# Index scores from the longest row of keys to the shortest, with each mask added at its tile

## The reference, cut to what matters

```python
logits = jnp.einsum('bqhd,bkd->bqhk', qi, k_idx_f)
score = jnp.einsum('bqh,bqhk->bqk', wi, jax.nn.relu(logits))
score = jnp.where(s_pos[None, None, :] <= t_pos[None, :, None], score, -jnp.inf)
_, idx = lax.top_k(score, topk)
```

## Time and profile before

| | us |
|---|---|
| median of 3 runs | 3659.33 (3657.73 to 3661.23) |
| the profiled execution, its own time | 3661.77 |
| the profiled execution, span of the trace | 3660.0 |
| TensorE busy in the span | 3364.4 |
| VectorE busy in the span | 1764.8 |

### The profile page before, as it was taken

How to read it: one execution, slowest core, us unless ns; L and a number is a source line. 1 busy time by engine, 2 the same in 40 slices (tenths; PEclk the granted TensorE clock), 3 DMA queues, 4 the chain that set the end, 5 groups by cost and what they waited for, 6 DMA issues and landing times. The chain is left out here.

```text
span 3660.0 us, 39794 instructions
## 1 busy us (share of the span) xinstructions
PE 3364.4 (92%) x15224; PEld 2696.9 (74%) x15224; DVE 1764.8 (48%) x2726; ACT 1115.5 (30%) x1955; POOL 579.7 (16%) x401
## 2 busy tenths in 40 slices
PE   7999888876989899999999998988899899999998
PEld 5776666665777587888888776776666688888886
DVE  4425544457341435555554539789543423242334
ACT  4323333325232322122111424136675321111212
POOL 0002365642100001010000200000164201000010
PEclk8999999988999999999999999999999999999999
DMA  4232323230321004332221301123233111111111
GB/s 122 75 101 84 118 78 115 87 134 15 117 68 65 37 20 133 98 97 97 97 80 48 133 18 41 46 56 84 67 67 114 39 58 47 46 52 50 47 46 58
DMA packets 223493, 270.27 MB, mean 74 GB/s; under 512 B 17259, under 2 KB 150276, under 8 KB 221298
## 3 DMA queue, kind: packets, MB, share of 16 engines
q1 hardware_dynamic: 223348, 268.30, 23.6%
HBM read 219.68 MB, written 29.18 MB: 68 GB/s over the span
## 5 line engine op out<-in xcount | busy, mean ns | idle before, releaser
L193 PE MATMUL psum<-rounded,rounded 128*128 128x512 f32 (+2 forms) x3936 | 1540.7, 391 | 115.6 <-DVE rounded L222 51.3
L194 PE MATMUL psum<-rounded,rounded 128*128 128x512 f32 (+2 forms) x3936 | 1530.5, 389 | 0.0
L195 PE MATMUL psum<-rounded,rounded 128*128 128x512 f32 (+2 forms) x3936 | 1529.1, 388 | 0.0
L193 PEld LDWEIGHTS psum<-rounded,rounded 128*128 128x128 f32 x3936 | 748.1, 190 | 293.1 <-DVE rounded L222 56.5
L195 PEld LDWEIGHTS psum<-rounded,rounded 128*128 128x128 f32 x3936 | 747.7, 190 | 152.4
L194 PEld LDWEIGHTS psum<-rounded,rounded 128*128 128x128 f32 x3936 | 749.0, 190 | 148.8 <-issue 0.2
L2966 DVE TENSOR_TENSOR plain<-psum,plain 128x512 f32<-128x512 f32 x432 | 288.2, 686 | 110.7 <-PE psum L195 109.1
L2977 DVE TENSOR_TENSOR plain<-psum,plain 128x512 f32<-128x512 f32 x44 | 30.4, 691 | 424.1 <-ACT plain L2881 424.1
L3538 POOL TENSOR_TENSOR plain<-plain,plain 128x128 f32<-128x128 f32 (+3 forms) x64 | 96.9, 1523 | 591.4 <-ACT plain L3636 516.0
L3343 DVE TENSOR_SCALAR_CACHE_REDUCE plain<-plain,plain 128x384 bf16<-128x384 f32 (+2 forms) x204 | 181.8, 942 | 1.3
L2958 DVE TENSOR_TENSOR rounded<-plain,rounded 128x512 fp32r<-128x512 f32 x108 | 97.2, 900 | 164.8 <-ACT rounded L2870 164.6
(11 more groups left out here) (327 smaller groups left out, 3467.1 us busy)
## 6 DMA issues: line engine op xcount, KB each, us to landing
plain<-in_ff_w_dram SPq DMA_DIRECT2D x64, 512.0 KB, 5.4
plain<-in_w_ada_dram SPq DMA_DIRECT2D x96, 256.0 KB, 3.3
plain<-in_w_gu_dram SPq DMA_DIRECT2D x44, 512.0 KB, 4.9
plain<-in_w_in_dram SPq DMA_DIRECT2D x36, 512.0 KB, 4.0
rounded<-rounded SPq DMA_DIRECT2D x72, 256.0 KB, 3.4
plain<-in_c_fwd_dram SPq DMA_DIRECT2D x64, 256.0 KB, 2.6
plain<-in_w_down_dram SPq DMA_DIRECT2D x22, 512.0 KB, 3.7
fold<-plain SPq DMA_DIRECT2D x8, 1024.0 KB, 5.0
```

Source lines behind the costliest of these rows:

```text
L193: nc.tensor.matmul(out, wh, xh, start=first, stop=False)
L194: nc.tensor.matmul(out, wh, xl, start=False, stop=False)
L195: return nc.tensor.matmul(out, wl, xh, start=False, stop=last)
```

## The change

The list of steps runs over the tiles from 7 down to 2. The zeros and the mask of tiles 0 and 1 are written by VectorE at the block's start, before it waits for the heads' weights. The mask of each other tile is added right behind its eighth head, after a wait for that head's addition.

```diff
-    steps = [(i, h) for i in range(FIRST_SEL, TT) for h in range(8)]
+    steps = [(i, h) for i in reversed(range(FIRST_SEL, TT)) for h in range(8)]
...
         @block.vector
         def _(dve):
+            for i in range(FIRST_SEL):
+                sc = sel_tile(core, i)
+                if i:
+                    nc.vector.memset(sc[:, 0:i * P], 0.0)
+                nc.vector.tensor_copy(sc[:, i * P:], core.small[:, 4, :])
             dve.wait_ge(S["tr_done"].sem, S["tr_done"].at(1))
...
                 ins.then_inc(S["dve_done"].sem, 1)
-            dve.wait_ge(S["dve_done"].sem, S["dve_done"].at(len(steps)))
-            for i in range(TT):
-                sc = sel_tile(core, i)
-                if i < FIRST_SEL:
-                    if i:
-                        nc.vector.memset(sc[:, 0:i * P], 0.0)
-                    nc.vector.tensor_copy(sc[:, i * P:], core.small[:, 4, :])
-                else:
+                if h == 7:
+                    dve.wait_ge(S["dve_done"].sem, S["dve_done"].at(n + 1))
                     nc.vector.tensor_tensor(sc[:, i * P:], sc[:, i * P:], core.small[:, 4, :], ALU.add)
```

## The result

| | before | changed |
|---|---|---|
| median of 18 runs, us | 3662.44 (3657.15 to 3667.61) | 3667.79 (3665.67 to 3670.16) |
| profiled execution, its own time / span, us | 3661.77 / 3660.0 | 3667.50 / 3665.7 |

The ratio is 1.0016, with an interval from 1.0010 to 1.0023: the change costs 3.7 to 8.4 us, 5.3 by the medians, where 2.4 were forecast. With 18 runs the kernel before has a median 3.1 us above that of the three runs on which the prediction stood; its runs are 10 us apart, so that the forecast of an absolute time was narrower than its base.

A forecast was written before the change was run, and what follows sets the result against it. VectorE's chain was taken to bound the index-score stage. Ramp +1.8, passages +1.9, tail -1.3 and TensorE's clock 0 made +2.4 us on a median of 3659.33: 3661.7 us, range 3657.3 to 3665.0.

The forecast's parts named there:

- What bounds the stage: Index-score stage: VectorE's chain sets its length; TensorE starts the next stage 1.21 us behind VectorE's last mask.
- Ramp: Start of the index-score stage: VectorE's chain gets going later with 1024 keys first, +1.8 us (bounds 0.5 and 2.6).
- The first two parts: At the stage's start: 1.08 us more until the first relu begins, 0.53 more for the relu itself.
- The lateness of the second step: At the stage's start: the second relu ends late, so VectorE's next step begins 0.20 us later.
- Passages: Between tiles on VectorE: five masks with their waits cost 0.38 us each, +1.9 us (bounds 1.0 and 2.8).
- Tail: End of VectorE's chain: one mask left, 0.38 us instead of 1.68, -1.3 us (bounds -1.5 and -1.1).
- The pause: TensorE ahead of the next stage: idle 5.1 us instead of 9.21, clock still 0.50 at restart, 0 us gained.
- my bound: Behind TensorE's pause: half clock lasting 5.6 us instead of 4.6 would cost 0.5 us.
- The signs of failure: VectorE idle between steps, matmuls behind the pause 0.23 us apart, or short tiles at a clock under 1.00.
- the last sentence of the rivals: Something outside the stage wins over 7.3 us: no mechanism seen, all behind it only shifts by 2.4 us; 2%.
- the upper end: Whole kernel: 3665.0 us, from the dear bounds, +4.8 us, and about 0.9 for the spread of the runs.
- The chances: Whole kernel: 94% within 0.2%, 4% slower by over 0.2%, 2% faster; the forecast itself 80%.

The follow-up runs named there:

- order_only: The kernel before with only the list of steps turned round (tile 7 first), all masks still behind the 48th step: 3661.79 us, ratio 1.0002.
- after_fill370: The changed kernel with two matmuls that nobody reads in TensorE's pause near 2370 us, one either side of the hand-over: 3665.71 us, 1.0009 to the kernel before.
- after_late_masks: The changed kernel with each mask moved behind the next tile's head-0 step, the last mask at the end: 3661.59 us, 1.0000 to the kernel before.
- after_plus_11: The changed kernel with one addition over 1024 keys that nobody reads behind VectorE's last mask: 3666.02 us, 1.0009 to the kernel before.
- short_first_fill: Against the kernel before: tiles 2, 7, 6, 5, 4, 3, masks one instruction later, five unread matmuls behind the last score: 3659.06 us, again 3658.56.
- before_fill: The kernel before with eight matmuls that nobody reads behind TensorE's last score: 3661.39 us, ratio 1.0000.

## Why the prediction was wrong, step by step

- **What bounds the stage: right.** VectorE's chain set the stage's length in every trace; TensorE restarted 1.21 us behind the last mask again (2236.87 - 2235.66).
- **Ramp: 1.8 forecast, 1.6 measured.** The first two parts, 1.6, were right. The lateness of the second step that I had added, 0.20, wasn't there: the first addition starts 0.86 us after the head-0 step, without idle time. order_only shows the term by itself.
- **Passages: 1.9 forecast, 1.6 measured.** The mask starts 0.03 us behind the addition, not 0.10. A passage cost 0.32 us, where my row gave 0.38. The Trainium skill says in "VectorE: DVE Perf Modes", section "The DRAIN you can't avoid", that a semaphore costs nothing extra between two VectorE instructions. By that rule a passage would have been 0.28; 0.32 lies between, nearer to the rule.
- **Tail: -1.3 forecast, -1.35 measured.** The writes of tiles 0 and 1 were covered, as forecast. The chain's sum was 2.4 and is 1.9.
- **The pause: right in size (5.1 forecast, 5.04), and the clock was at half when it ended.** That half clock lasts as long behind the shorter pause was wrong; it went from 4.5 to 6.1 us behind the restart, because the same 10.24 us at half clock began 0.90 us into the pause instead of 3.50. That is the 0.7 us under "restart", 0.2 beyond my bound, though one of my own rows (5.6 us behind a pause of 4.99) pointed that way.
- **The signs of failure.** None of the three that the prediction names came: VectorE had no idle time between steps, the matmuls behind the pause started 0.43 apart, and the short tiles ran at 1.00. All three look at the stage and its pause, and none at what lies behind.
- **The step that failed** is the last sentence of the rivals, "all behind it only shifts by 2.4 us", on which the sum and the upper end rest. What lies behind doesn't only shift: whether the clock falls at a pause of TensorE there depends on when the pause comes. In the changed kernel the one near 2370 us went to half clock and cost 2.9 us, and several others changed by 0.8 in balance. Where 2.4 stood in the sum, the trace has 1.9 in the stage, 0.7 behind its pause, 2.9 near 2370 and 0.8 later, 6.3 in all. That this is cause and not coincidence is shown for 2370 by after_fill370, which differs by two matmuls at that pause and takes 1.9 us less in the median (2.9 in the trace; the intervals of the two ratios overlap), and for the moment at which the stage ends by after_late_masks and after_plus_11: a stage 1.6 us shorter and one 1.1 us longer both lose the surplus.
- **The chances.** The change lies within 0.2%, as forecast, but the measured time is 2.8 us above the range and 6.1 above the forecast: 3.1 of these are owed to the base, three runs for a kernel whose runs are 10 us apart, and 3.0 to the terms and steps above.

For the pause near 2370 the time since the clock's last rise orders what the traces show; why the clock falls on one side of that place and not on the other is open, and so is the balance of 0.8 us at the pauses behind it. Nor is it settled how often each kernel goes either way, since one execution of each was traced (two of the changed one and two of short_first_fill, which agree).

## What to carry to other kernels

A stage bound by one engine's chain can be costed from its ramp, its passages and its tail to within half a microsecond, but in a kernel whose TensorE pauses many times the time of the whole moves by a few microseconds more, up or down, with any edit that shifts what follows; so read the traces' lateness place by place before a small difference is put down to the edit. Start a chain of this kind with a short row, put small dependent work behind an instruction that doesn't need it, and fill TensorE's pause with matmuls that nobody reads: with 1.20 to 1.41 us left (four traces) the clock stayed full, with 2.15 us left it fell.

## What the hardware showed that I had not expected

The same pause of 2.75 us ended at clock 1.00 in one kernel and at 0.50 in another, 14 matmuls at 0.43 us instead of 0.23, and 1.1 us of extra work on VectorE 135 us earlier made the difference. The pause began 127.60 us behind the clock's last rise where it ended at half clock, and 128.21 where it ended at full. A shorter pause (5.04 us) was followed by more work at half clock (6.1 us) than a pause of 9.21 us (4.5 us), because the clock fell 0.90 instead of 3.50 us into it and stayed at half for 10.24 us both times. In before_fill the clock was still full at the restart and fell 1.2 us into dense work.
